# Latent attention heads: which engine evicts which transposes, where the first head's transposes stand, and layer inputs kept in DRAM

## The reference

```python
h = rms_norm(x, norm_g) * (1.0 + scale[:, None, :]) + shift[:, None, :]
proj = h @ w_in
c_q, c_kv, k_pe, na_qkv, diff_qkv, g_mla, g_na, g_diff = jnp.split(proj, IN_SPLITS, axis=-1)

q = (rms_norm(c_q, q_lat_g) @ w_uq).reshape(B, S, MLA_HEADS, MLA_QK)
kv = (rms_norm(c_kv, kv_lat_g) @ w_ukv).reshape(B, S, MLA_HEADS, MLA_NOPE + MLA_V)
k_nope, v_mla = kv[..., :MLA_NOPE], kv[..., MLA_NOPE:]
k = jnp.concatenate([k_nope, jnp.broadcast_to(k_pe[:, :, None, :], (B, S, MLA_HEADS, MLA_ROPE))], axis=-1)
q = rms_norm(q, mla_q_g)
k = rms_norm(k, mla_k_g)
...
o_mla = blocked_attention(q, k, v_mla, MLA_QK ** -0.5).reshape(B, S, MLA_WIDTH)
...
y = jnp.concatenate([o_mla * jax.nn.silu(g_mla),
                     o_na * jax.nn.silu(g_na),
                     o_d * jax.nn.silu(g_diff)], axis=-1) @ w_out
return x + gate[:, None, :] * y
```

## Time and profile before

| What | us |
|---|---|
| median of three timed runs | 3917.64 |
| profiled execution, its own time | 3922.74 |
| profiled execution, span from first to last instruction | 3920.8 |
| TensorE busy | 3792.8 (97%) |
| VectorE busy | 2644.9 (67%) |
| ScalarE busy | 1928.5 (49%) |
| GpSimd busy | 667.7 (17%) |

### The profile page before, as it was taken

How to read it: one execution, slowest core, us unless ns; L and a number is a source line. 1 busy time by engine, 2 the same in 40 slices (tenths; PEclk the granted TensorE clock), 3 DMA queues, 4 the chain that set the end, 5 groups by cost and what they waited for, 6 DMA issues and landing times.

```text
span 3920.8 us, 52203 instructions
## 1 busy us (share of the span) xinstructions
PE 3792.8 (97%) x21022; PEld 2891.3 (74%) x21022; DVE 2644.9 (67%) x3273; ACT 1928.5 (49%) x2784; POOL 667.7 (17%) x731
## 2 busy tenths in 40 slices
PE   8999999999999999999999889999999999999999
PEld 6875567787875567787853568888888888888887
DVE  4436967675436967534435563889889868898898
ACT  5336865424336865424346443544545654444454
POOL 0120111101130111102048841000000340000010
PEclk9999999999999999999999999999999999999999
DMA  4112000252112000032100001111112101211111
GB/s 186 60 41 52 1 1 12 76 208 94 49 51 52 1 1 9 25 118 77 44 22 1 25 33 65 47 68 58 43 54 75 44 33 54 76 43 54 65 54 65
DMA packets 57232, 209.70 MB, mean 53 GB/s; under 512 B 14368, under 2 KB 15008, under 8 KB 44960
## 3 DMA queue, kind: packets, MB, share of 16 engines
q1 hardware_dynamic: 41648, 150.25, 10.9%
q10 hardware_dynamic: 15344, 56.11, 4.0%
HBM read 189.56 MB, written 12.58 MB: 52 GB/s over the span
## 4 chain that ended last, share of the span: by engine, by line
PE 87%; DVE 7%; ACT 3%; issue 2%; POOL 1%; DMA 0%; ACTq 0%; DVEq 0%; POOLq 0%
PE ps L1676 34%; PE ps L969 15%; PE ps L1385 3%; PE ps L1209 3%; PE ps L1211 3%; PE ps L1210 3%; PE ps L1075 2%; PE ps L1438 2%; PE ps L1427 2%; PE ps L1340 2%; PE ps L1326 1%; PE ps L1356 1%; PE ps L1092 1%; PE ps L1481 1%; PE ps L1080 1%
## 5 line engine op out<-in xcount | busy, mean ns | idle before, releaser
L1676 PE MATMUL ps<-x_piece1hi,w_piece1hi 128*128 128x512 f32 x672 | 262.4, 390 | 0.2 <-DVE x_piece1lo L3420 0.2
L1676 PE MATMUL ps<-x_piece0hi,w_piece0hi 128*128 128x512 f32 x672 | 262.3, 390 | 0.0
L1676 PE MATMUL ps<-x_piece0lo,w_piece0hi 128*128 128x512 f32 x672 | 261.5, 389 | 0.0
L1676 PE MATMUL ps<-x_piece0hi,w_piece0lo 128*128 128x512 f32 x672 | 261.4, 389 | 0.0
L1676 PE MATMUL ps<-x_piece2hi,w_piece2lo 128*128 128x512 f32 x672 | 261.4, 389 | 0.0
L1676 PE MATMUL ps<-x_piece1lo,w_piece1hi 128*128 128x512 f32 x672 | 261.4, 389 | 0.0
L1676 PE MATMUL ps<-x_piece1hi,w_piece1lo 128*128 128x512 f32 x672 | 261.4, 389 | 0.0
L1676 PE MATMUL ps<-x_piece2hi,w_piece2hi 128*128 128x512 f32 x672 | 261.4, 389 | 0.0
L1676 PE MATMUL ps<-x_piece2lo,w_piece2hi 128*128 128x512 f32 x672 | 261.4, 389 | 0.0
L969 PE MATMUL ps<-n_hi_m,w_lo 128*128 128x512 f32 x608 | 238.6, 392 | 0.0
L3926 POOL TENSOR_TENSOR rope_cos<-rope_cos,arena 128x512 f32<-128x512 f32 x42 | 65.5, 1559 | 735.5 <-ACT arena L2399 732.4
(11 more groups left out here) (489 smaller groups left out, 10438.5 us busy)
## 6 DMA issues: line engine op xcount, KB each, us to landing
w<-in_wstream SPq DMA_DIRECT2D x87, 1024.0 KB, 4.9
arena<-in_wstream SPq DMA_DIRECT2D x40, 1024.0 KB, 4.9
arena<-in_wstream ACTq DMA_DIRECT2D x16, 1024.0 KB, 5.2
out<-h ACTq DMA_DIRECT2D x32, 256.0 KB, 2.6
h<-in_na_bias ACTq DMA_DIRECT2D x6, 1152.0 KB, 5.6
h<-in_xT SPq DMA_DIRECT2D x2, 2048.0 KB, 17.6
m<-in_wstream SPq DMA_DIRECT2D x4, 1024.0 KB, 17.2
h<-in_xT ACTq DMA_DIRECT2D x4, 1024.0 KB, 10.4
```

Of the source, the lines that this page charges most:

```text
L1676: last = mm(dst[:, e, :], a_part[:, pair, k, f], b_part[:, k, :], start=(n in FRESH and half == 0 and k == 0 and t == 0), stop=(half == 1 ...
```

## The change

Three things change in both layers.

1. **The "pe" groups.** Next to the weight block's high part, VectorE now lays out 64 columns for each of the 8 tiles: the 32 high and the 32 low columns of the rotary key. One pass with these against the high input and one against the low input replace three passes: 16 products for a group, not 24. The two halves of 32 output rows are added by the table product that used to copy them (`picks`, now over 64 rows), for which the table gets one more copy.
2. **The input in DRAM.** SyncE stores the eight tiles of `n_hi_m` in a DRAM tensor during the projection, one behind each of eight weight blocks, and loads them to `n_hi_h` in the latent loop. `n_lo` stays where it is. GpSimd's additions and subtractions and ScalarE's roundings are gone.
3. **The latent loop.** In steps 1 to 23 the first head's transposes stand directly behind the scores. ScalarE evicts them, ahead of its exponentials; VectorE evicts the second head's, behind the output copy.

```diff
+PE_AT = KT * (KVL + MLA_ROPE) + 64
-LAT_GATE_ORDER = (0, 1, 2, 3, 6, 7, 8, 9, 10, 11, 4, 5, 12, 13, 14, 15)
-LAT_GATE_AT = {6: (0,), 7: (1,), 9: (2,), 10: (3,), 18: (4, 5, 6), 19: (7, 8, 9), 20: (10, 11, 12), 21: (13, 14, 15)}
+LAY_SPLIT = 16 * KT + 16
+        saved = nc.dram_tensor("n_saved", (P, KT, S), F32).ap()
...
+            def input_save(layer, k):
+
+                sp.wait_ge(sems["x_hi"], H2 * KT * (layer + 1))
+                sp.wait_ge(sems["lay_split"], LAY_SPLIT * layer)
+                sp.dma_start(saved[:, k, :], n_hi_m[:, k, :].bitcast(F32)).then_inc(sems["restored"], 16)
+
+            def input_back(layer, tiles):
+                sp.wait_ge(sems["restored"], 16 * KT * (layer + 1))
+                for k in tiles:
+                    sp.dma_start(n_hi_h[:, k, :].bitcast(F32), saved[:, k, :]).then_inc(sems["lay_split"], 16)
+
             for j in range(2, len(STREAMED)):
+                layer, b = divmod(j, LAYER_STREAMED)
                 if j in DIFFERENTIAL_AT:
                     differential_loads(DIFFERENTIAL_AT[j])
                 streamed(j)
+                if layer < L and 2 <= b < 2 + KT:
+                    input_save(layer, b - 2)
+                if j in DIFFERENTIAL_AT:
+                    input_back(layer, (0, 1, 3))
+                    sp.wait_ge(sems["lat_ready"], LAT_C * (layer + 1))
+                    input_back(layer, (4, 5, 6, 7))
+                    sp.wait_ge(sems["o_full"], (NA_STEPS + DF_STEPS + LAT_STEPS) * (layer + 1) - LAT_STEPS + LAT_AT_LAST + 1)
+                    input_back(layer, (2,))
...
+                        if g.kind == "pe":
+                            for k in range(KT):
+                                both = pe_home[:, PE_AT + 64 * k - 64:PE_AT + 64 * k + 64]
+                                for x in (hi, n_lo):
+                                    last = mm(ps[:, i % 4, :], both, x[:, k, g.hf * HALF:g.hf * HALF + HALF],
+                                              start=(k == 0 and x is hi), stop=(k == KT - 1 and x is n_lo))
+                            last.then_inc(sems["acc_ready"], g.inc)
...
                 for s in range(LAT_STEPS + 2):
                     if s < LAT_STEPS:
                         latent_scores(layer, s)
+                    if 1 <= s <= LAT_STEPS - 1:
+                        if s == 1:
+                            pe.wait_ge(sems["lat_d_act"], 10 * layer + 6)
+                        latent_probs_t(layer, 2 * s - 2)
...
-                    if 1 <= s <= LAT_STEPS:
-                        if s == 1:
-                            pe.wait_ge(sems["lat_d_act"], 10 * layer + 6)
+                    if s == LAT_STEPS:
                         latent_probs_t(layer, 2 * s - 2)
...
-            def gate_input(layer, i):
...
                 for s in range(LAT_STEPS + 1):
                     p = LAT_AT.get(s)
+                    if s:
+                        latent_pt(layer, 2 * s - 2)
                     if s < LAT_STEPS:
                         latent_exp(layer, 2 * s)
...
-                    if s:
-                        latent_pt(layer, 2 * s - 1)
-                    for u in LAT_GATE_AT.get(s, ()):
-                        gate_input(layer, u)
...
+                if pe_columns:
+                    dve.wait_ge(sems["v_link"], T.next("v_link"))
+                    both = home[s][:, PE_AT:PE_AT + 64 * KT].rearrange("p (k n) -> p k n", k=KT)
+                    for i, part in enumerate((home[s], w_lo[s])):
+                        from_ = part[:, 0:KT * (KVL + MLA_ROPE)].rearrange("p (k n) -> p k n", k=KT)[:, :, KVL:]
+                        last = V.tensor_copy(both[:, :, 32 * i:32 * i + 32], from_.bitcast(F32))
+                    last.then_inc(sems["w_split"], 1)
...
-                    if 1 <= s <= LAT_STEPS:
-                        latent_pt(layer, 2 * s - 2)
                     if s >= 2:
                         latent_out(layer, s - 2)
+                    if 1 <= s <= LAT_STEPS:
+                        latent_pt(layer, 2 * s - 1)
...
-                for k in RESTORED:
-                    G.tensor_tensor(out=n[:, k, :], in0=n_lo[:, k, :].bitcast(F32), in1=n_hi_m[:, k, :].bitcast(F32),
-                                    op=ALU.add).then_inc(sems["restored"], 1)
```

66 lines of the change are left out of this document (22 added, 44 removed).

## The result

| | before | changed |
|---|---|---|
| median of the timed runs | 3917.97 us (4 runs, 3914.71 to 3920.04) | 3944.72 us (4 runs, 3939.87 to 3946.76) |
| ratio | | 1.0067 (95%: 1.0054 to 1.008) |
| profiled execution, span | 3920.8 us | 3945.0 us |
| first scores to last transposes, first loop | 204.1 us | 221.0 us |
| the same, second loop | 204.1 us | 223.6 us |

The change makes the kernel 0.67% slower, +26.75 us. The forecast was +14 and its range ended at 3942, so the sign was right and the size was not. In the profiled executions the two loops together are 36.4 us longer, the two projections up to the attention's first products 6.7 us shorter (2.5 and 4.2), and all else is 5.5 us shorter.

The account below looks back on a forecast made before the run. The prediction took TensorE, busy for 97% of the span at full clock, as the bound. The loops' +10.8 us a layer, twice +21.6, less 7.2 for the projections, gave +14.4 us: 3932 us, range 3916 to 3942.

Parts of the forecast that it names:

- query steps: Latent loop steps with long input products for a query chunk: 9.43 against 8.82 us, +3.8 us a layer.
- key steps: Latent loop steps with short input products for a key chunk: 8.06 against 7.85 us, +1.1 us a layer.
- steps into 8 and 16: Scores that wait for VectorE's rotation of the next head pair's queries: 1.93 us later each, +3.9 us a layer.
- step 3 to 4: Loop step with two more products on VectorE and no room left for them: later exponentials, +1.4 us a layer.
- last steps, 18 to 23: Second head's transposes lose a 0.82 us wait, but the next scores need both exponentials: -0.8 us a layer.
- gate products, end of loop: Step 24: gate products need the half weight block that VectorE rounds behind its eviction: +1.4 us a layer.
- two new chains: Loop: with the exchanged evictions, ScalarE's first exponential comes 0.66 us late and VectorE's low part 1.93 us later.
- Rival (a): Loop: the intended effect wins, TensorE sees only the freed waits; -20 us, 3897 us, chance 0.07.
- (b): Loop: only the single waits remain, 5.9 us a layer; +4.6 us, 3922 us, chance 0.12.
- (d): Loads of the inputs from DRAM hold a weight block: +10 us, 3942 us, chance 0.08.
- (e): The order in the loop is indifferent and only the saved products count: -7.2 us, 3910 us, chance 0.06.
- Rival (c): GpSimd's four subtractions a loop held VectorE up to 1.28 us each, removal returns it: +4 us, 3922 us, chance 0.05.

Follow-up runs that it names:

- the DRAM part alone: Kernel before with only the inputs kept in DRAM (stores and loads instead of additions, subtractions and copies): 3917.86 us, ratio 0.9998.
- the loop alone: Kernel before with only the new order of the latent loop and the exchanged evictions: 3959.87 us, ratio 1.0102.
- the kernel with the rotation first: Changed kernel with VectorE's eviction of the second head's transposes behind the rotation, in steps that have one: 3931.09 us, ratio 1.0031.
- the kernel with only T1 moved: Kernel before with the first head's transposes directly behind the scores, each eviction on its old engine and in its old place: 3918.77 us, ratio 1.0004.
- the one with the saved products alone: Kernel before with only the 64-column weights of the pe groups: 3909.20 us, ratio 0.9973.

## Why the prediction was wrong, point by point

| term, a layer | predicted | measured |
|---|---|---|
| query steps | 9.43 us | 9.40, and 9.41 with waits filled |
| key steps | 8.06 us | 8.03 |
| exponentials after the scores | 4.73 us | 4.71 |
| steps into 8 and 16 | +1.93 each | +1.63 each (11.79 less 10.16) |
| step 3 to 4 | +1.4 | +1.1 (9.09 less 7.96) |
| last steps, 18 to 23 | -0.8 | -0.2 |
| gate products, end of loop | +1.4 | +1.5 at full clock, +2.9 and +3.1 as it ran |
| a loop | +10.8 | +11.2 at full clock, +16.9 and +19.5 as it ran |
| projections, both layers | -7.2 | -6.7 in the profile, -10.8 (uncertain by 4) alone |
| inputs in DRAM | 0 | 0 in the old order |

**The step that failed** is a sentence ahead of the sum: "TensorE's own work is unchanged, so what decides is whether the two new chains fit." Its number of products is unchanged; their duration is not. The earlier trace rows has full clock over the loop, and I took that as a property of the kernel, with the earlier trace rows beside it, whose slices of 98 us are too coarse for it (the kernel before has 103 us of half clock in all, none of it in the loops): "a microsecond of TensorE's work or waiting is worth about one of the total". It is a property of a loop in which TensorE hardly waits. The prediction then put waits of over 2 us in front of the scores of steps 8 and 16 and of the gate products, named the first two among its signs, and priced each at its length. Behind them the products ran at the 1.2 GHz level, and that cost another 1.3 to 2.9 us each time, 8.5 us at steps 8 and 16 and 3.0 at the gate products; with the falls in steps 1 to 3 of the second loop it makes 14 us (5.7 in the first loop, 221.0 less 215.3, and 8.3 in the second, 223.6 less 215.3). 21.6 and 14 are the 36.4 us of the two loops, to within 1 us. That idling is the cause is shown for steps 8 and 16: filling the wait or shortening it took the fall away at all four, and lengthening it in the kernel before brought it at all four. For the other 5.7 us (gate products, and steps 1 to 3) the half clock is seen, but equal waits at these places also passed without it, and why is open.

The Trainium skill ("TensorE: Matmul & The Clock Gate", section "Part 1: The HAM clock gate (the "warmup" mystery)") says that the chip sets TensorE's clock by how busy TensorE has been of late, and that it is halved after idling. The kernels with filled waits agree with it: the same lateness, products in place of idling, and 1.00 instead of 0.50 at steps 8 and 16. The prediction did not weigh that page.

**What was right.** Both chains: the 4.7 us of ScalarE's, and its effect of 0.6 and 0.2 us a step; VectorE's late rotation; step 3; the end of the loop. That the loop's sum at full clock comes within 0.4 us is in part luck: the rotation and step 3 cost 0.9 us a loop less than I had, the last steps and the step from 1 to 2 some 1.1 more. One sign missed: ahead of the scores of steps 8 and 16 I had over 3 us of waiting, and it was 2.32 (2.72 for the weight loads). Rival (a) is refuted, and by a stronger argument than mine: even without any chain in its way, T1's earlier place frees no wait. Rivals (b), (d) and (e) are refuted by the steps, by the DRAM part alone (it costs nothing), and by the loop alone (the order is anything but indifferent).

**Rival (c)** had 0.05 and was half right. I judged that GpSimd's subtractions were free because the steps with one are no longer than those without. That holds for the order of before, and the run without them confirms it. In the new order they cost 2.4 us a loop (the loop alone), by just the mechanism that I had set aside, and ScalarE's copies cost 0.7. So the DRAM part repairs some 6 us of a damage that only the loop's part of the same change makes. In the changed kernel one such collision is left, in the step from 1 to 2: 9.93 us instead of the 9.43 that I had for it, the +0.53 us of GpSimd's addition (1.26 less 0.73). In the kernel with the rotation first the two do not meet, the addition takes 0.73 and the step 9.41.

**What came out of single executions.** All else in the changed kernel's profile was 5.5 us shorter than in that of before. I first took it for a gain of the DRAM part in the attentions. But the kernel with only T1 moved, whose code there is that of before, is 5.6 us shorter between the loops as well: the profiled execution of before had more half clock there (34.1 us against 27.3), which is part of it. The rest of the sum in the medians: 36.4 less 7.2 is +29.2, against +26.75 (ratio's interval: +21 to +31).

## What to carry to other kernels

When a change puts a new wait of some microseconds on TensorE in a loop that it bounds (here 2.3 us and more), price it twice: once for its length, and once for what may run at half clock behind it. Here the second price was about as large as the first (1.3 to 2.9 us behind waits of 2.3 to 3.0), and it was paid at most of these places, not at all. Two ways out were seen: reorder the engine that is waited for so that the wait is short (13.6 us here), or keep TensorE busy in the wait with products that nobody reads, which only pays where TensorE is the bound. And a piece of work that is free in one order need not be free in the next: the same GpSimd subtraction cost nothing before the exchange and 0.9 us behind it. Of all versions run, the one with the saved products alone had the lowest median, 3909.20 us, 0.27% under the kernel before.

## What the runs showed of the hardware

TensorE's granted clock fell to 0.5 behind single waits in a loop that otherwise kept it busy, but not behind each. Ahead of the scores of steps 8 and 16 it fell at all 12 waits of 2.32 to 3.98 us that were not filled (three kernels), and at none of 1.26. Ahead of the gate products, with 2.45 us, it fell in 6 of 8 loops; in step 1, with 2.45 or 2.98 us, in 4 of 10, and with 1.41 us in 7 of 16. So the length of the wait alone does not decide it, and no run here shows what else does.

How long it stayed down differed too: the four waits of 2.32 us in the changed kernel were followed by steps that were 1.6, 2.8, 2.8 and 1.3 us too long. The falls behind step 1 mostly show in the step from 2 to 3 (8.96 to 9.58 us for 7.9 to 8.0, in one or both loops of seven kernels, and 10.22 in the second loop of the changed one), so single executions differ there by 1.0 to 2.2 us, also where no edit is near.

A VectorE operation on two operands in SBUF, 0.42 us alone, took 1.37 to 1.50 us beside a GpSimd subtraction of 1.28 us, and a GpSimd addition of 0.73 us took 1.26 beside two VectorE products: whichever started second took longer.
